# A two-block float32 network on one core: merged 512-column products in the expert slabs, scores moved among the query slabs, and VectorE work reordered

## The reference, cut to what matters

```python
q = (xb @ w_q).reshape(tokens, 8, 2, 128)            # 8 heads, 2 halves
s = einsum('thcd,hckd->thck', q, sub_keys)           # 128 keys each
s1, i1 = top_k(s[:, :, 0], 16); s2, i2 = top_k(s[:, :, 1], 16)
top_s, pos = top_k(s1[..., :, None] + s2[..., None, :], 16)
eidx = i1 * 128 + i2 at pos;  gate = softmax(top_s)
h = gelu(einsum('thkd,td->thk', u[eidx], xb))
y = einsum('thk,thkd->td', gate * h, v[eidx])        # u, v: 16384 experts x 1024
```

## Time and profile before

| | us |
|---|---|
| three runs | 2248.54, 2248.08, 2246.60; median 2248.08 |
| the profiled execution | 2247.95 |
| its span in the profile | 2246.1 |
| TensorE busy in the span | 2219.6 (99%) |
| VectorE, ScalarE, GpSimd busy | 1490.1, 1231.0, 1123.1 |
| TensorE's granted clock, mean | 0.998 |

### The profile page before, as it was taken

One profiled execution on the slowest core, in us unless ns is written; L12 is line 12 of the kernel. 1 busy time (PEld: TensorE's weight loads), 2 busy tenths in 40 slices (PEclk: granted clock), 3 DMA queues, 4 the chain that ended last, 5 costly groups with the idle time before them and its releaser, 6 DMA issues.

```text
span 2246.1 us, 42878 instructions
## 1 busy us (share of the span) xinstructions
PE 2219.6 (99%) x15104; PEld 2037.3 (91%) x15104; DVE 1490.1 (66%) x2876; ACT 1231.0 (55%) x1925; POOL 1123.1 (50%) x494
## 2 busy tenths in 40 slices
PE   8999999999999999999999999999999999999998
PEld 6997988999999999998888889899999999888886
DVE  5432763433697777777777764459877777777777
ACT  4545644444547888853333346445688886333332
POOL 6878449588688777740000025668877775000000
PEclk9999999999999999999999999999999999999999
DMA  6645436356455455465556654545554455556654
GB/s 206 241 160 179 160 113 200 131 185 216 144 185 183 162 162 162 159 211 192 193 193 210 195 175 136 172 155 178 183 167 162 159 166 200 195 192 192 212 192 129
DMA packets 109645, 399.05 MB, mean 178 GB/s; under 512 B 12752, under 2 KB 13136, under 8 KB 108752
## 3 DMA queue, kind: packets, MB, share of 16 engines
q1 hardware_dynamic: 104688, 380.16, 51.7%
q10 hardware_dynamic: 4832, 17.17, 2.3%
HBM read 394.13 MB, written 3.15 MB: 177 GB/s over the span
## 4 chain that ended last, share of the span: by engine, by line
PE 95%; DVE 2%; issue 1%; POOL 1%; ACT 1%; DMA 0%; ACTq 0%; DVEq 0%; POOLq 0%; SPq 0%
PE G L446 18%; PE G L448 18%; PE G L447 18%; PE XX L448 11%; PE XX L446 11%; PE XX L447 11%; PE XX L876 1%; PE XX L878 1%; PE G L513 1%; POOL w_lo L2299 1%; PE G L506 1%; PE G L500 1%; PE XX L855 1%; PE XX L787 0%; DMA ring<-slabs_in 0%
## 5 line engine op out<-in xcount | busy, mean ns | idle before, releaser
L2299 POOL TENSOR_TENSOR w_lo<-ring,w_hi 128x1024 fp32r<-128x1024 f32 (+1 forms) x468 | 1115.1, 2406 | 770.3 <-ACT w_hi L1093 769.7
L1093 ACT ACTIVATE w_hi<-ring 128x1024 fp32r<-128x1024 f32 x722 | 745.5, 1056 | 592.7 <-PE XX L448 408.5
L446 PE MATMUL G<-hT_hi,w_hi 128*128 128x256 f32 x2816 | 806.1, 286 | 0.8 <-POOL w_lo L2299 0.8
L447 PE MATMUL G<-hT_lo,w_hi 128*128 128x256 f32 x2816 | 796.3, 283 | 0.0
L448 PE MATMUL G<-hT_hi,w_lo 128*128 128x256 f32 x2816 | 796.2, 283 | 0.0
L446 PEld LDWEIGHTS G<-hT_hi,w_hi 128*128 128x128 f32 x2816 | 539.6, 192 | 1.6 <-POOL w_lo L2299 1.0
L447 PEld LDWEIGHTS G<-hT_lo,w_hi 128*128 128x128 f32 x2816 | 539.8, 192 | 0.3
L448 PEld LDWEIGHTS G<-hT_hi,w_lo 128*128 128x128 f32 x2816 | 539.5, 192 | 0.0
L446 PE MATMUL XX<-w_hi,hT_hi 128*128 128x512 f32 x1024 | 398.5, 389 | 0.0
L448 PE MATMUL XX<-w_hi,hT_lo 128*128 128x512 f32 x1024 | 398.4, 389 | 0.0
L447 PE MATMUL XX<-w_lo,hT_hi 128*128 128x512 f32 x1024 | 398.4, 389 | 0.0
(11 more groups left out here) (320 smaller groups left out, 2511.6 us busy)
## 6 DMA issues: line engine op xcount, KB each, us to landing
ring<-slabs_in SPq DMA_DIRECT2D x722, 512.0 KB, 4.6
big<-rows_in ACTq DMA_DIRECT2D x10, 512.0 KB, 6.3
big<-rows_in ACTq DMA_DIRECT2D x3, 1024.0 KB, 8.1
big<-keys_in ACTq DMA_DIRECT2D x2, 1024.0 KB, 7.2
h_kept<-h ACTq DMA_DIRECT2D x2, 1024.0 KB, 10.0
h<-h_kept ACTq DMA_DIRECT2D x2, 1024.0 KB, 7.6
big<-ws_in ACTq DMA_DIRECT2D x1, 1024.0 KB, 8.3
out<-h SPq DMA_DIRECT2D x4, 256.0 KB, 2.0
```

The costliest lines, as they stand in the source:

```text
L446: nc.tensor.matmul(out, a_hi, b_hi, start=start, stop=False, skip_group_check=True)
L447: nc.tensor.matmul(out, a_hi, b_lo, start=False, stop=False, skip_group_check=True)
L1093: nc.scalar.activation(w_hi[:, 2 * j + half, 0:n], ring[j][:, half * 1024:half * 1024 + n], ACT.Copy).then_inc(hi_ready, 1)
L2299: Q.tensor_tensor(w_lo[:, 2 * j + half, 0:n], ring[j][:, half * 1024:half * 1024 + n], w_hi[:, 2 * j + half, 0:n], ALU.subtract).then_inc( ...
```

## The change

It has five parts. (1) u slabs 21 to 63 use `project_merged`: hi*hi and hi*lo become one matmul with 512 moving columns, since `hT_hi` and `hT_lo` now lie beside each other, and a half's products are sorted by kind: 8 with 512 columns, then 8 of `w_lo` with 256. A slab so fills a pair of banks, two partial results side by side; ScalarE copies the second part to SBUF (`addend`), VectorE adds it to the first (`sum_parts`), and gelu follows. Two pairs are used in turn. (2) The 8 tiles of scores are spread: 4 after query slab 4, 2 after slab 6, 2 after u slab 0; VectorE ranks each part when it comes. (3) The gates start at slab 20 over 42 slabs instead of slab 23 over 39. (4) `hot2` is four operations that each compare and multiply in one, and every third `hot1` is one comparison on VectorE. (5) VectorE's orders in `a_v`, `r_v` and "m". The diff, cut:

```diff
-GATED = 23
-SPAN = 39
+GATED = 20
+SPAN = 42
+MERGED = 21
+SCORES = [(0, 0), (0, 1), (1, 0), (1, 1), (0, 2), (1, 2), (0, 3), (1, 3)]
-        hT_hi = sb("hT_hi", [P, DC, T], f32r)
-        hT_lo = sb("hT_lo", [P, DC, T], f32r)
+        hT_both = sb("hT_both", [P, DC, 2, T], f32r)
+        hT_hi, hT_lo = hT_both[:, :, 0, :], hT_both[:, :, 1, :]
...
+            def project_merged(l, n):
+                s, pair = SLAB0[f"u{l}"] + n, pair_of(l, n)
...
+                    pe.wait_ge(*pair_taken(l, n))
+                for half in range(2):
+                    q = half_ready(s, 0, half)
+                    parts = [(4 * half + i, a, slice(i * 256 + a * P, i * 256 + (a + 1) * P)) for i in range(4) for a in range(2)]
+                    for c, a, w in parts:
+                        nc.tensor.matmul(GG[pair][:, a, :], w_hi[:, q, w], hT_both[:, c, :, :].rearrange("p s t -> p (s t)"),
+                                         start=c == 0, stop=False, skip_group_check=True)
+                    for c, a, w in parts:
+                        last = nc.tensor.matmul(GG[pair][:, a, 0:T], w_lo[:, q, w], hT_hi[:, c, :], start=False,
+                                                stop=c == DC - 1, skip_group_check=True)
+                    last.then_inc(half_done, 1)
...
-                project_slab(SLAB0[f"pq{l}"] + 7, 0, hT, DC, False)
+                project_slab(SLAB0[f"pq{l}"] + 4, 0, hT, DC, False)
                 pe.wait_ge(sem(f"keys_loaded{l}"), 16)
                 x_read(pe, f"p_qt{l}")
-                for i in range(8):
...
+                for i in range(4):
+                    scores(i)
+                for n in range(5, 7):
+                    project_slab(SLAB0[f"pq{l}"] + n, 0, hT, DC, False)
+                for i in range(4, 6):
+                    scores(i)
+                project_slab(SLAB0[f"pq{l}"] + 7, 0, hT, DC, False)
...
-            take_wide("a_v", A_v, (0,), {2: mix_weights, 3: rotary_tables, 5: rates_and_rows, 7: other_rows})
+            take_wide("a_v", A_v, (0,), {2: mix_weights, 5: tables_and_rows, 7: rates_and_rows})
...
                 def hot1(x):
+                    if x % 3 == 2:
+                        return
...
+                def copy_part(n):
+                    if n >= MERGED:
+                        act.wait_ge(half_done, 2 * (SLAB0[f"u{l}"] + n + 1))
+                        act.wait_ge(sem(f"summed{l}"), n - MERGED)
+                        nc.scalar.activation(addend[:, :, :], parts_of(l, n)[1], ACT.Copy).then_inc(sem(f"part_copied{l}"), 1)
                 for n in range(GATED, GATED + SPAN):
+                    split_half(SLAB0[f"u{l}"] + n + RING, 0)
+                    copy_part(n)
+                    split_half(SLAB0[f"u{l}"] + n + RING, 1)
                     gelu_in_place(n, n)
-                    split(SLAB0[f"u{l}"] + n + RING)
...
                         split(SLAB0[f"u{l}"] + n + RING)
+                    copy_part(n)
                     gelu_in_place(n, n)
...
-            dve.wait_ge(sem("pos_loaded"), 16 * 4)
+            def turns_of_angles():
...
+            def angles_within_pi():
...
                 V.tensor_copy(A_v[:, 1, g * 512:(g + 1) * 512], tile[:, :]).then_inc(free, 1)
-                if g == 2:
+                if g == 0:
+                    turns_of_angles()
+                if g == 1:
+                    angles_within_pi()
+                if g == 3:
                     decay_rates()
...
-            for i in range(8):
-                r_v_rest(i)
+                for n in ((0, 1), (2, 3), (), (4, 5, 6, 7))[i]:
+                    r_v_rest(n)
...
+                top_scores(0, (0, 1))
+                top_scores(1, (2, 3))
+                top_scores(0, (4,))
+                top_scores(1, (5,))
+                top_scores(0, (6,))
+                top_scores(1, (7,))
...
-                    link(V.tensor_tensor(chosen, bc(counting, 1, 4), bc(picksT[:, 1, t], 2, NKEYS), ALU.is_equal))
-                    V.tensor_tensor(hot[:, 3 + x % 2, :, :], chosen, bc(gate16[:, 0, t], 2, NKEYS), ALU.mult)
-                    V.tensor_tensor(hot[:, 5 + x % 2, :, :], chosen, bc(gate16[:, 1, t], 2, NKEYS), ALU.mult
-                                    ).then_inc(sem(f"hot2_{l}"), 1)
+                    for q in range(4):
+                        t = 4 * x + q
+                        last = V.scalar_tensor_tensor(hot[:, 3 + x % 2:7:2, q, :], bc(counting, 1, 2), picksT[:, 1, t:t + 1],
+                                                      bc(gate16[:, :, t], 2, NKEYS), ALU.is_equal, ALU.mult)
+                    last.then_inc(sem(f"hot2_{l}"), 1)
...
+                def sum_parts(n):
+                    if n >= MERGED:
+                        first = parts_of(l, n)[0]
+                        dve.wait_ge(sem(f"part_copied{l}"), n - MERGED + 1)
+                        V.tensor_tensor(first, first, addend[:, :, :], ALU.add).then_inc(sem(f"summed{l}"), 1)
...
                 for n in range(GATED, GATED + SPAN):
-                    times_gelu(n)
-                    for x in groups_of(n):
+                    sum_parts(n)
+                    if n < MERGED:
+                        times_gelu(n)
+                    for i, x in enumerate(groups_of(n)):
                         times_gates(x)
                         if x + 2 < GROUPS:
                             hot2(x + 2)
+                        hot1(x + 3)
+                        if i == 0 and n >= MERGED:
+                            times_gelu(n)
                 x_read(dve, f"p_w{l}")
                 for n in range(GATED + SPAN, 63):
+                    sum_parts(n)
                     times_gelu(n)
...
+                sum_parts(63)
                 times_gelu(63)
...
-            attention("m", False, float(P + ROPE) ** -0.5, m_unit, m_rest, {3: [0], 5: [1], 7: [2, 3]})
+            attention("m", False, float(P + ROPE) ** -0.5, m_unit, m_rest, {4: [0], 6: [1], 7: [2, 3]})
```

More of the change, by code:

```diff
@@ L834, in experts, with scores @@
                           lambda i: x_read(pe, f"p_tr{l}", i))
-                for n in range(2, 7):
+                def scores(i):
+                    b, part = SCORES[i]
+                    for s in (SLAB0[f"pq{l}"] + 2 * part, SLAB0[f"pq{l}"] + 2 * part + 1):
+                        pe.wait_ge(g_free[s % 4], tiles_before(s) + 1)
+                    tile = x_begin(f"p_s{l}", i)
+                    for a in range(4):
+                        hc = 4 * part + a
+                        last = nc.tensor.matmul(tile[:, a * P:(a + 1) * P], K_q[:, hc, b * P:(b + 1) * P],
+                                                keysT[:, hc, :], start=True, stop=True)
+                    last.then_inc(x_full, 1)
+                for n in range(2, 4):
                     project_slab(SLAB0[f"pq{l}"] + n, 0, hT, DC, False)
@@ L1410, in experts, with take_query_columns, take_scores @@
                 split_half(SLAB0[f"pq{l}"] + RING, 1)
-                for n in range(7):
+                def take_query_columns():
+                    for i in range(2):
+                        tile, free = x_tile(act, f"p_qt{l}", i)
+                        nc.scalar.activation(flat(K_q[:, 2 * i:2 * i + 2, :]), tile[:, :], ACT.Copy).then_inc(free, 1)
+                def take_scores(tiles):
+                    for i in tiles:
+                        b, part = SCORES[i]
+                        tile, free = x_tile(act, f"p_s{l}", i)
+                        nc.scalar.activation(flat(K_s[:, b, 4 * part:4 * part + 4, :]), tile[:, :], ACT.Copy
+                                             ).then_inc(free, 1)
+                for n in range(8):
                     if n:
@@ new lines, in angles_within_pi @@
+            def angles_within_pi():
+                src = 0
+                for part in (6.28125, 0.0019350051879882812, 3.019916050561733e-07):
+                    link(V.scalar_tensor_tensor(R_a[:, 2, :], R_a[:, 1, :], -part, R_a[:, src, :], ALU.mult, ALU.add))
+                    src = 2
+                link(V.tensor_scalar(R_a[:, 3, :], R_a[:, 2, :], np.pi / 2, None, ALU.add))
+                link(V.tensor_scalar(R_a[:, 1, :], R_a[:, 3, :], np.pi, -2 * np.pi, ALU.is_gt, ALU.mult))
+                link(V.tensor_tensor(R_a[:, 3, :], R_a[:, 3, :], R_a[:, 1, :], ALU.add))
+                V.tensor_scalar(R_a[:, 2:4, :], R_a[:, 2:4, :], 3.1415925, -3.1415925, ALU.min, ALU.max
+                                ).then_inc(sem("angles"), 1)
```

166 lines of the change are left out of this document (101 added, 65 removed).

## The result

| | time, us | ratio to before, 95% interval |
|---|---|---|
| before | 2247.34, median of 4 (2246.27 to 2248.54) | |
| after | 2231.49, median of 4 (2228.94 to 2232.11) | 0.9927 (0.9914 to 0.9941) |
| forecast | 2224.0 (2217 to 2235) | |

The account below looks back on a forecast made before the run. TensorE, busy 99% of the span, was taken as the bound; -18.4 - 6.8 - 1.2 - 1.3 + 0.5 + 2.4 + 1.0 = -23.8 us from 2247.95 gave 2224, range 2217 to 2235.

Parts of the forecast that it names:

- A: Rival for the u slabs: the merge brings almost nothing, 2.3 us saved, time 2240; chance 0.06.
- C: Rival in the gated stretch: `sum_parts` takes VectorE's slow form, 2.2 instead of 0.7 us; +59 us, time 2283; chance 0.04.
- B: Rival: next waits take the gains ahead of the experts, the seam costs 3 us a layer; time 2234.5; chance 0.14.
- the doubles: Gated stretch: where two slabs with two groups follow each other, the second `hot2` ends about when due; +0.5 us, both layers.
- Merging a pair saves 13.4 ns: Merged u slabs: one 512-column product takes 226.2 ns against 239.6 for two of 256; -18.4 us over 86 slabs.
- Attention m, -1.3: Attention m: a later `m_rest` removes VectorE's 1.65 us delay, another may delay unit 5 by 0.7; bounds 0 and -3.1.
- The seam, +1.2 a layer: From u to v: later split and roundings make the first `hT_lo` end at 6.7, slab 63 at 5.5; +2.4 us in all.
- just in time: Seam: four `hT_lo` delay the last sum, gelu 63 and the third v slab's rounding, which was found still due in time.
- `a_v`, -6.8: Stage `a_v`: copies ahead of the angles remove TensorE's 5.66 us stand and low clock, -8.3, less +1.5; bounds -8.3 and -4.
- ScalarE's chain of the rates: `a_v`: decay rates move to the end, behind the row loads, when splits are due; +1.5 us of a possible 4.1.
- `r_v`: Stage `r_v`: TensorE's 1.2 us wait goes as the first two `R_vl` no longer stand behind four maps; -1.2 us.
- Gates, doubles and scores: More switches between kinds of product on TensorE, +1.0 us, and successive slabs with two groups, +0.5, both layers together.

Follow-up runs that it names:

- run 2: Changed kernel with a half slab's products not sorted by kind, each 512-column product followed by its 256-column one: 2236.24 us, ratio 0.9952.
- run 12: Changed kernel with both m and seam mends, and merged products sorted by kind over the whole slab instead of each half: 2224.55 us, ratio 0.9899.
- run 3: Changed kernel with products still sorted by kind, but the first bank's four chunks ahead of the second's: 2231.22 us, ratio 0.9930.
- run 6: Changed kernel with `m_rest(0)` back at unit 3 and the rotated key in m copied by one instruction instead of two: 2225.61 us, ratio 0.9906.
- run 8: Changed kernel with the two rows of the norm issued after slab 3 of `a_v` instead of slab 5: 2230.70 us, ratio 0.9927.
- run 7: Changed kernel with first keys rounded before slab 62's second split half and slab 63 summed behind the second `hT_lo`: 2228.93 us, ratio 0.9921.

## Why the prediction was right, and where its sum was off

The mechanism was right: TensorE is the bound, a merged slab takes less of its time, and nothing beside it (pairs, `hot2`, the sum, the picks) became a wait of more than 0.05 us. Of the rivals, A (2.3 us from the merge) is out by the 13.8 measured, and C by the sum's 697 ns in the midst of GpSimd's work. B came true in m, whose gain the next wait took and more; but `a_v` lost 0.4 us and not 4.3, and a seam cost 1.5 and not 3. The sum missed 8 us, in two terms of 4.6 and 4.3, with small ones on both sides.

That the time still lies within the range is in part luck. The merge had no bound of its own but the -18.4, and m was bounded at 0: both measured worse than the worst case that the range was added up from. The room came from `a_v`, the seam and the doubles, whose bounds weren't used up.

**"Merging a pair saves 13.4 ns", 18.4 us in all.** It measured 86 x 0.16 = 13.8. I took the pace of 226.2 ns from the v stage, where every product has 512 columns and the run never ends. In the u stage the products come in runs of eight, and a run begins with steps of 225 to 236 ns before it comes to 226; with a run of one (run 2) they stay at 232 to 241, with a run of sixteen (run 12) most are 226 or 227. Besides, the step behind the 16-bit gates is 87 ns over a product's own, against 82 before. So 16 products of 512 cost 3.68 us without that step's surplus, not 3.62. The remaining 16 of 256 run at 119 and give 0.01 back. That makes 0.05 us a slab, the difference of 0.214 and 0.16. What in the engine makes a run begin unevenly isn't known; only that the order and the length of the runs change it, and the bank (run 3) doesn't.

**"Attention m, -1.3".** It measured +3.0 in the changed kernel. I had seen that one `m_rest` could delay a unit, and bounded it "between 0 and -3.1", nothing on the side of a loss. I asked what VectorE's later work does to the unit, and not which tile `m_rest(0)` frees: the next transposes write it. That made a stop of 2.6 us where the order of before has 1.8 and 0.7, and the lower clock behind it cost another 1.7: 1.5 us in all by the stages. The other 1.5 us are the collision of run 6, which I had no means to foresee: it needs the phase of two engines to 0.3 us.

**The seam, +1.2 a layer.** It measured 1.5. The first stop came as I said, for the first `hT_lo` (0.54 us); the second, for the third v slab, I had found "just in time", and it was 0.8 late.

**`a_v`, -6.8.** It measured -6.4 in the profiled execution, and from -5.6 to -8.1 in the ten with that order of loads. The 5.66 us and the low clock of the earlier trace rows did go. But what came next was not ScalarE's chain of the rates, as I had it: the stop stands at 62.1, and the chain begins at 63.85. It was a slab that landed at 58.6, while the rows of the norm were loaded beside it; with the rows earlier (run 8) the stop came earlier.

**The rest.** `r_v` gave 1.6 against 1.2. Gates, doubles and scores cost 0.1 a layer in the changed kernel against 0.75 (the table's 6.5 us up to slab 62 against 41 x 0.16), which gave 1.3 back and hid a part of what the merge lacked. The new one-hot form takes 478 ns against the 0.48 us interpolated from the earlier trace rows.

## What to carry to other kernels

A product's price taken from a stage where nothing else runs was too low here for a stage that alternates sizes: read it from runs of the same length, or keep the larger figure as the range's other end, and let runs of one kind be long. When an order is moved, write down for each moved instruction what it frees, as well as what it makes and what it waits for; the `m_rest` that frees a ring tile cost more than the one that was in the way had cost. A small copy beside another engine's long instruction can be held for the whole of that: one instruction instead of two leaves half as many places where it can happen.

## What the runs showed of the hardware that I had not expected

A run of products of 512 columns (fp32r, new weights for each) does not begin at its settled pace: the steps are 225, 230, 236, 229, 232, 231, 227 ns in the first run of a slab and 233, 236, 229, 232, 231, 227, 226 in the second, the same in every slab. They never come down to their columns at 2.4 GHz (226.5 against 213.3). At the lower level the products of 256 columns do come to theirs at 1.2 GHz: behind the stop at 62.1 they start 213 ns apart, as here from 64.03 on (five steps in 1.06 us), against 120 and not 106.7 at the upper.

```profile
64.03 0.41 PE L472 MATMUL GG<-hT_both,w_hi 128*128 128x256 f32 x1
...
65.09 0.41 PE L474 MATMUL GG<-hT_both,w_lo 128*128 128x256 f32 x1
```

The Trainium skill, page "TensorE: Matmul & The Clock Gate", section "Back-to-back issue gap", gives for an isolated matmul about 2.5 ns over the columns at the upper level and none at the lower. The lower agrees here (213 ns), the upper doesn't for these products (120 and 226.5 ns, 13 over their columns).

The same stop of 2.6 us at the same place had a granted clock of 0.66 for five us behind it in one kernel and of 1.00 in another (run 7), whose earlier stages were only some 2.4 us ahead. That is 1.7 us more or less for the same stop, and a difference of this size between two kernels may come from it alone. Of the six profiled executions with this stop, five had the lower clock.

The code of `a_v` and `a_u` took up to 2.4 us more or less in ten profiled executions of it, where the later stages repeat within 0.1 but for the stop in m. In the changed kernel it is the one stretch in which the DMA share stays near 1.00 for ten us (50 to 60), and TensorE waits there for a slab.
